# A diagonal of reciprocal roots in the opening, and a quarter of the first weights ahead of the last x tile

## The chip, the cores and the metric

The kernel runs on one core of one Trainium2 chip. The metric is the device time of one execution in microseconds; the median of three runs of the kernel before is 443.52 us (443.51 to 444.15).

## What is computed

A decoder layer on 512 tokens of width 1024, in float32. It begins with an RMSNorm and one wide projection, to which the change belongs:

```python
def rmsnorm(x, g):
    xf = x.astype(jnp.float32)
    y = xf * lax.rsqrt(jnp.mean(xf * xf, axis=-1, keepdims=True) + RMS_EPS)
    return (y * g.astype(jnp.float32)).astype(x.dtype)

h = rmsnorm(x, norm_g)
proj = jnp.einsum('bsd,dc->bsc', h, w_in)
```

Behind it stand dilated window attention for three groups of four heads, block-sparse attention for eight heads, gates, two branch projections, an output projection, a residual add and a last RMSNorm.

## The kernel before

Tokens lie in four x tiles of 128 rows (`TT` = 4). The projection wants them turned, as eight pieces of 128 channels by 512 tokens (`KT_D` = 8). Each operand of a projection is kept as a high part, rounded to the matmul's fast float32 form, and a low part, the rest; a product is three matmuls: high by high (L766), high by low weights (L767), low by high (L770). For the x side the parts are `hT_hi` and `hT_lo`, for the weights `w_hi` and `w_lo`.

The program is written engine by engine; each engine runs its instructions in the written order and waits on counters. A `link` is an instruction behind which the same engine waits for its own result.

The opening. SP issues the loads: the four x tiles (L570), the first chunk of weights in two column halves of 128 (L617, L618), then whole chunks of 256 columns (L620) into three buffers `raw`. ScalarE's queue loads 24 small vectors into `vecs` (the norm's gains and the biases). GpSimd makes the unit matrix `ident`, then eight instructions of distance constants (L666 to L683: iota and select), and then works on the first weights: rounding of rows 0 to 3 of the eight k pieces (L690), of rows 4 to 7 (L691), the low part of the latter (L693), the rounding of step 1 (L697). TensorE runs 14 full float32 matmuls of `ident` (L738), each of them two records in the trace.

For each x tile ScalarE sums the squares (L1010; of the last tile only the lower half, the upper is VectorE's, L1219), VectorE takes mean and reciprocal (L1205, L1206, L1228, L1230), ScalarE the root (L1015), and then the tile is scaled in place by that number per row: tiles 0 and 1 by VectorE (L1200), of tiles 2 and 3 the lower half by ScalarE (L1020) and the upper by VectorE. TensorE turns the scaled tile with eight transposes against `ident` (L750) into the PSUM banks. The vectors are turned by one transpose (L755) behind tile 0's; VectorE copies them out as `gb` and halves the biases into `hbias` (L1210, L1211). When tile 3 is turned, ScalarE writes `hT_hi` piece by piece (L1034), scaled by the gains, and VectorE `hT_lo` (L1241). Before that, VectorE makes the low part of k pieces 0 to 3 of the first weights (L1236).

The projection goes in steps of 128 columns, 24 matmuls of 512 columns each (L766 to L770), or for the values 48 of 256 (L816 to L818, two steps sharing their weights). Steps 0 and 1 are keys, 2 and 3 queries, 4 and 5 values. ScalarE rounds the weights of a step from step 2 on (L990), two steps ahead; GpSimd makes their low part (L662); ScalarE and VectorE take a finished key step (L1049, L1264) or query step (L1049, L1259). A load into a buffer waits until both parts of the chunk in it are made. From step 6 on attention work stands between the steps. VectorE finishes the constants with five instructions (L1437 to L1441) before its first step.

Of the kernel before, what the change touches and what calls it, by code (L numbers as in the profile page):

```python
# [29 lines left out]
F32 = mybir.dt.float32  # L30
# [6 lines left out]
P = 128  # L37
# [50 lines left out]
HALVED = 2  # L88
WARM = 14
NRING = 4  # L90
SKEW = 8
# [189 lines left out]
def hybrid_layer_program(nc, x, norm_g, w_in, b_merge, w_pa, w_pb, w_out, final_g, out):  # L281
    stats_dram = nc.dram_tensor("stats_by_position", (SEQ, NDIL * 8), F32, kind="Internal").ap()
    top = ExitStack()
    with top:
# [25 lines left out]
        ss_part = sb("ss_part", [P, 2], F32)  # L310
# [3 lines left out]
        rvar = sb("rvar", [P, TT], F32)  # L314
# [17 lines left out]
        squares = sb("squares", [P, TT, D], F32, xstack)  # L332
        xstack.close()
# [57 lines left out]
        first_half_in = [sem(f"first_half_in{i}") for i in range(2)]  # L391
# [5 lines left out]
        var_ready = sem("var_ready")  # L397
        rstd_ready = sem("rstd_ready")
        x_scaled = sem("x_scaled")
        x_scaled_low = sem("x_scaled_low")  # L400
# [66 lines left out]
        def raw_waits(item, half=0):  # L467

            if item == ("w", 0):
                return first_half_in[half], 16  # L470
# [97 lines left out]
        def _(sp):  # L568
            for i in range(TT):
                sp.dma_start(xs[:, i, :], x_t[:, i, :]).then_inc(x_in[i], 16)  # L570
            def place_values(u):

                V = V_odd if u % 2 else V_even
                sp.wait_ge(v_rows_ready, 2 * u)
                sp.wait_ge(valued, HU * (u - 1))
                for t in range(TT):
                    sp.dma_start(V[32 * t:32 * t + 32, :, :],
                                 V_rows[:, t, :]).then_inc(v_placed, 16)
# [10 lines left out]
            for n, (k, c) in enumerate(LOADS):  # L589
# [51 lines left out]
        def _(pool):  # L641
# [13 lines left out]
            def lows(n):  # L655
# [3 lines left out]
                if n >= NRING:  # L659
# [8 lines left out]
            link(nc.gpsimd.affine_select(out=d_full[:], in_=d_full[:], compare_op=ALU.is_ge, fill=BIG, base=384,  # L668
                                         pattern=[[-1, 512]], channel_multiplier=1))

            band = d_band[:].rearrange("p (a c) -> p a c", a=2)
            link(nc.gpsimd.iota(band, [[0, 2], [-1, 256]], base=P, channel_multiplier=1,
                                allow_small_or_imprecise_dtypes=True))
            link(nc.gpsimd.affine_select(out=band, in_=band, compare_op=ALU.is_ge, fill=BIG, base=P,
                                         pattern=[[0, 2], [-1, 256]], channel_multiplier=1))
            link(nc.gpsimd.affine_select(out=band, in_=band, compare_op=ALU.is_ge, fill=BIG, base=0,
                                         pattern=[[0, 2], [1, 256]], channel_multiplier=-1))

            link(nc.gpsimd.iota(d_quad[:], [[-4, P]], base=0, channel_multiplier=4,
                                allow_small_or_imprecise_dtypes=True))  # L680
            link(nc.gpsimd.affine_select(out=d_quad[:], in_=d_quad[:], compare_op=ALU.is_ge, fill=BIG, base=0,
                                         pattern=[[-1, P]], channel_multiplier=1))
            nc.gpsimd.iota(d_hex[:].bitcast(I32), [[-1, P]], base=0, channel_multiplier=1).then_inc(consts_ready, 1)  # L683
            pool.wait_ge(consts_ready, 2)

# [9 lines left out]
            pool.wait_ge(first_half_in[1], 16)  # L695
            src, kt = raw_half(1)
            nc.gpsimd.tensor_copy(ring(w_hi, 1, kt), src).then_inc(hi_ready, 1)  # L697

# [34 lines left out]
        def _(pe):  # L733
# [6 lines left out]
            for i in range(TT):  # L740
                if i < HALVED:
                    pe.wait_ge(x_scaled, i + 1)
                else:
                    pe.wait_ge(x_scaled_low, i - HALVED + 1)
                for k in range(KT_D):
                    if i >= HALVED and k == KT_D // 2:
                        pe.wait_ge(x_scaled, i + 1)
                    if i == 1 and k == 7:
                        pe.wait_ge(gb_ready, 1)
                    last = pe.transpose(ps[:, k, P * i:P * i + P], xs[:, i, P * k:P * k + P], ident[:, :])  # L750
                    if i == TT - 1:
                        last.then_inc(x_turned, 1)
                if i == 0:
                    pe.wait_ge(vec_in, 32)
                    pe.transpose(ps[:, 7, SEQ - 24:SEQ], vecs[:, :], ident[0:24, 0:24]).then_inc(vecs_turned, 1)  # L755
# [225 lines left out]
        def _(act):  # L981
# [26 lines left out]
            def square_rows(i, n):  # L1008
                act.wait_ge(x_in[i], 16)
                nc.scalar.activation(squares[:, i, 0:n], xs[:, i, 0:n], ACT.Square,  # L1010
                                     accum_out=ss[:, i:i + 1]).then_inc(squared, 1)

            def root(i):
                act.wait_ge(var_ready, i + 1)
                nc.scalar.activation(rstd[:, i:i + 1], rvar[:, i:i + 1], ACT.Sqrt).then_inc(rstd_ready, 1)  # L1015

            def scale_low_half(i):
                act.wait_ge(rstd_ready, i + 1)
                half = xs[:, i, 0:D // 2]
                nc.scalar.activation(half, half, ACT.Copy, scale=rstd[:, i:i + 1]).then_inc(x_scaled_low, 1)  # L1020

            for i in range(HALVED):
                square_rows(i, D)
                root(i)
            square_rows(2, D)
            square_rows(3, D // 2)
            for i in range(HALVED, TT):
                root(i)
            for i in range(HALVED, TT):
                scale_low_half(i)  # L1030
# [158 lines left out]
        def _(dve):  # L1189
# [8 lines left out]
            def scale_rows(i, at):  # L1198
                dve.wait_ge(rstd_ready, i + 1)
                nc.vector.tensor_scalar(xs[:, i, at:], xs[:, i, at:], rstd[:, i:i + 1], None,  # L1200
                                        ALU.mult).then_inc(x_scaled, 1)

            def variance(i):
                dve.wait_ge(squared, i + 1)
                link(nc.vector.tensor_scalar(var[:, i:i + 1], ss[:, i:i + 1], 1.0 / D, EPS, ALU.mult, ALU.add))  # L1205
                nc.vector.reciprocal(rvar[:, i:i + 1], var[:, i:i + 1]).then_inc(var_ready, 1)  # L1206

            def turn_vectors():
                dve.wait_ge(vecs_turned, 1)
                link(nc.vector.tensor_copy(gb[:], ps[:, 7, SEQ - 24:SEQ]))  # L1210
                nc.vector.tensor_scalar(hbias[:], gb[:, 8:24], 0.5, None, ALU.mult).then_inc(gb_ready, 1)  # L1211

            for i in range(HALVED):
                variance(i)
                scale_rows(i, 0)
            turn_vectors()
            last, high = TT - 1, slice(D // 2, D)
            dve.wait_ge(x_in[last], 16)
            link(nc.vector.scalar_tensor_tensor(out=squares[:, last, high], in0=xs[:, last, high], scalar=1.0,  # L1219
                                                in1=xs[:, last, high], op0=ALU.mult, op1=ALU.mult,  # L1220
                                                accum_out=ss_part[:, 0:1]))
            nc.vector.tensor_scalar(ss_part[:, 1:2], ss_part[:, 0:1], 1.0 / D, EPS, ALU.mult,
                                    ALU.add).then_inc(dve_chain, 1)
            chain[0] += 1
            variance(last - 1)
            dve.wait_ge(dve_chain, chain[0])
            dve.wait_ge(squared, last + 1)
            link(nc.vector.scalar_tensor_tensor(out=var[:, last:TT], in0=ss[:, last:TT], scalar=1.0 / D,  # L1228
                                                in1=ss_part[:, 1:2], op0=ALU.mult, op1=ALU.add))
            nc.vector.reciprocal(rvar[:, last:TT], var[:, last:TT]).then_inc(var_ready, 1)  # L1230
# [301 lines left out]
```

## Time and profile before

| | |
|---|---|
| median of 3 runs | 443.52 us |
| the profiled execution, own time | 443.48 us |
| its span, first to last instruction | 441.7 us |
| TensorE busy | 431.6 us, 98% of the span |
| VectorE, ScalarE, GpSimd busy | 212.8, 198.5, 176.3 us |
| first projection matmul starts | 14.58 us |

In the views PE is TensorE's matmuls, PEld its weight loads, DVE VectorE, ACT ScalarE, POOL GpSimd, SPq SP's DMA issues; L738 is line 738 of the kernel. A timeline row gives the start in us from the span's start, the duration in us, engine, line, operation, destination <- sources, shapes and count, and in brackets how long the engine was idle before it and what ended that. A DMA's landing is the time from issue to the arrival of the last byte.

### The profile page before, as it was taken

To read this page: it belongs to the slowest core of one execution; us is meant where nothing else is said; L and a number is where in the kernel's file an instruction comes from. 1 tells how busy PE (TensorE), PEld (TensorE's weight loads), DVE (VectorE), ACT (ScalarE), POOL (GpSimd) and SP (SyncE) were. 2 spreads that over 40 slices of the span, in tenths; PEclk is the share of its full clock that TensorE was granted. 3 is DMA by queue.
4 is the path that set the end of the run, shared out by engine and by line. 5 is a ranking of instruction groups with operands and counts; after the bars stand their busy time and mean duration, and the time that the engine had idled before them with its cause. 6 is when DMAs were issued, how large, how long until landed. Compare 5 with 4: busy or idle time off the path is not lost.

```text
span 441.7 us, 6258 instructions
## 1 busy us (share of the span) xinstructions
PE 431.6 (98%) x2377; PEld 374.5 (85%) x2377; DVE 212.8 (48%) x367; ACT 198.5 (45%) x401; POOL 176.3 (40%) x113
## 2 busy tenths in 40 slices
PE   7899999999999999999999999999999999999995
PEld 6789998899889988988888888888888888888885
DVE  3831244344435446757857664827025173083334
ACT  5743555335544464567555554533223543332111
POOL 4744442243243333646499543534355354200000
PEclk9999999999999999999999999999999999999999
DMA  8962234622452263024122022222222284210421
GB/s 284 286 192 96 96 96 83 159 96 95 91 150 97 96 168 110 25 96 143 49 95 96 0 73 96 96 72 96 95 71 96 95 261 156 113 66 0 149 90 47
DMA packets 40044, 48.31 MB, mean 109 GB/s; under 512 B 3768, under 2 KB 35536, under 8 KB 40016
## 3 DMA queue, kind: packets, MB, share of 16 engines
q1 hardware_dynamic: 37568, 47.72, 34.4%
q10 hardware_dynamic: 2448, 0.21, 0.4%
q8 instruction: 19, 0.31, 0.3%
q14 instruction: 9, 0.07, 0.1%
HBM read 39.48 MB, written 2.15 MB: 94 GB/s over the span
## 4 chain that ended last, share of the span: by engine, by line
PE 96%; DMA 2%; DVE 1%; ACT 1%; SPq 0%; issue 0%; DVEq 0%; ACTq 0%
PE ps L766 20%; PE ps L770 20%; PE ps L767 20%; PE ps L816 4%; PE ps L818 4%; PE ps L817 4%; PE ps L890 3%; PE ps L974 3%; PE ps L975 3%; PE ps L973 3%; PE ps L873 3%; PE ps L917 3%; PE ps L907 2%; DMA xs<-in_x 2%; PE ps L865 1%; PE ps L850 0%
## 5 line engine op out<-in xcount | busy, mean ns | idle before, releaser
L662 POOL TENSOR_TENSOR w_lo<-raw,w_hi 128x1024 fp32r<-128x1024 f32 (+1 forms) x59 | 138.1, 2342 | 175.4 <-ACT w_hi L990 175.4
L766 PE MATMUL ps<-hT_hi,w_hi 128*128 128x512 f32 x336 | 135.0, 402 | 1.1 <-DVE hT_lo L1241 1.1
L770 PE MATMUL ps<-hT_lo,w_hi 128*128 128x512 f32 x336 | 131.2, 390 | 0.0
L767 PE MATMUL ps<-hT_hi,w_lo 128*128 128x512 f32 x336 | 131.1, 390 | 0.0
L770 PEld LDWEIGHTS ps<-hT_lo,w_hi 128*128 128x128 f32 x336 | 63.1, 188 | 13.5
L766 PEld LDWEIGHTS ps<-hT_hi,w_hi 128*128 128x128 f32 x336 | 63.2, 188 | 11.2 <-issue 1.3
L767 PEld LDWEIGHTS ps<-hT_hi,w_lo 128*128 128x128 f32 x336 | 63.3, 188 | 9.9
L990 ACT CAST w_hi<-raw 128x1024 fp32r<-128x1024 f32 (+1 forms) x58 | 59.2, 1020 | 8.3 <-PE ps L770 5.4
L816 PE MATMUL ps<-w_hi,hT_hi 128*128 128x256 f32 x160 | 45.6, 285 | 0.0
L818 PE MATMUL ps<-w_lo,hT_hi 128*128 128x256 f32 x160 | 44.7, 279 | 0.0
L817 PE MATMUL ps<-w_hi,hT_lo 128*128 128x256 f32 x160 | 44.6, 279 | 0.0
L704 POOL TENSOR_TENSOR probs<-probs,frec 128x128 f32<-128x128 f32 (+3 forms) x32 | 22.1, 722 | 23.7 <-DVE frec L1307 23.7
L1102 ACT ACTIVATE probs<-probs,stats 128x128 f32<-128x128 f32 (+1 forms) x48 | 20.1, 419 | 24.1 <-DVE stats L1366 24.1
L816 PEld LDWEIGHTS ps<-w_hi,hT_hi 128*128 128x128 f32 x160 | 30.2, 188 | 0.1
L817 PEld LDWEIGHTS ps<-w_hi,hT_lo 128*128 128x128 f32 x160 | 30.1, 188 | 0.1
L1076 ACT ACTIVATE gate<-ps,hbias 128x512 f32<-128x512 f32 x16 | 11.0, 690 | 42.7 <-PE ps L770 42.5
L818 PEld LDWEIGHTS ps<-w_lo,hT_hi 128*128 128x128 f32 x160 | 30.1, 188 | 0.0
L1102 ACT ACTIVATE probs<-probs,fmin 128x128 f32<-128x128 f32 (+3 forms) x32 | 17.9, 560 | 26.2 <-DVE fmin L1366 26.2
L1049 ACT ACTIVATE QTs<-ps 64x512 fp32r<-64x512 f32 x20 | 11.9, 593 | 25.6 <-PE ps L770 25.2
L1264 DVE TENSOR_TENSOR KTs<-ps,KTs 64x512 fp32r<-64x512 f32 x20 | 13.8, 688 | 19.0 <-ACT KTs L1049 18.7
L890 PE MATMUL ps<-ident,probs 128*128 128x128 f32 x140 | 21.4, 272 | 0.0
L1247 DVE TENSOR_TENSOR wo_a_lo<-raw,wo_a_hi 128x1024 fp32r<-128x1024 f32 x5 | 6.7, 1377 | 30.1 <-ACT wo_a_hi L1000 30.1
(148 smaller groups left out, 665.6 us busy)
## 6 DMA issues: line engine op xcount, KB each, us to landing
raw<-in_w_in SPq DMA_DIRECT2D x25, 1024.0 KB, 4.9
KTs<-KTs SPq DMA_DIRECT2D x20, 256.0 KB, 3.4
raw<-in_w_out SPq DMA_DIRECT2D x4, 1024.0 KB, 4.8
xs<-in_x SPq DMA_DIRECT2D x4, 512.0 KB, 5.3
raw<-in_w_pb SPq DMA_DIRECT2D x4, 512.0 KB, 4.1
res<-in_x SPq DMA_DIRECT2D x4, 512.0 KB, 3.9
out<-weighted SPq DMA_DIRECT2D x8, 256.0 KB, 2.1
raw<-in_w_in SPq DMA_DIRECT2D x2, 512.0 KB, 8.9
```

The source lines that it names most:

```text
L662: nc.gpsimd.tensor_tensor(ring(w_lo, n, kt), src, ring(w_hi, n, kt).bitcast(F32), ALU.subtract).then_inc(lo_ready, 1)
L704: nc.gpsimd.tensor_tensor(row, row, frec[:, h.n - NDIL * HU, i:i + 1].broadcast_to([P, n]), ALU.mult).then_inc(normed, 1)
L766: pe.matmul(out, wh, hh, start=(k == 0), stop=False)
L767: pe.matmul(out, wl, hh, start=False, stop=False)
L770: return pe.matmul(out, wh, hl, start=False, stop=(k == kts - 1))
L816: pe.matmul(o, hh, wh, start=(k == 0), stop=False)
L817: pe.matmul(o, hl, wh, start=False, stop=False)
L818: last = pe.matmul(o, hh, wl, start=False, stop=(k == KT_D - 1))
L890: last = pe.transpose(ps[:, TURN_BANKS[bank], P * b:P * b + P], probs[:, h.n % 2, at:at + P], ident[:, :])
L990: nc.scalar.copy(ring(w_hi, n, kt), src).then_inc(hi_ready, 1)
L1102: nc.scalar.activation(row, row, ACT.Exp, bias=nmin(h, i), scale=-1.0, accum_out=row_sum(h, i)).then_inc(exp_ready, 1)
L1264: nc.vector.tensor_tensor(lo, src, hi.bitcast(F32), ALU.subtract).then_inc(k_low, 1)
```

## The change

The x tiles are no longer scaled. Every tile's squares are split between ScalarE (lower half) and VectorE (upper half); VectorE turns its sum into a part of the mean, ScalarE takes the root with the other part as scale and that part as bias, VectorE takes the reciprocal and writes a matrix `diag` with it on the diagonal (for the last tile ScalarE writes it). TensorE turns and scales a tile at once by full float32 matmuls of the tile with `diag` in place of transposes with `ident`. The vectors are turned right behind the 14 matmuls, ahead of tile 0. Of tile 2 the last two pieces are turned between those of tile 3. The first column half of the first weights is loaded in two parts of four k pieces: one ahead of the last x tile, one behind it. GpSimd's distance constants are made behind the low part of step 2 instead of at the start, VectorE's five finishing instructions behind the taking of step 2.

```diff
@@ sync
+            def load_first_half(m):
+
+                ks = slice(FIRST_K * m, FIRST_K * m + FIRST_K)
+                at = CHUNKS[0][1]
+                dst = raw[:, 0, :].rearrange("p (k c) -> p k c", k=KT_D)
+                sp.dma_start(dst[:, ks, 0:P], w_in_t[:, ks, at:at + P]).then_inc(first_in[m], 16)
+
             for i in range(TT):
+                if i == TT - 1:
+                    load_first_half(0)
                 sp.dma_start(xs[:, i, :], x_t[:, i, :]).then_inc(x_in[i], 16)
+            load_first_half(1)
...
                     if n == 0:
-                        sp.dma_start(dst[:, :, 0:P], w_in_t[:, :, at:at + P]).then_inc(first_half_in[0], 16)
-                        sp.dma_start(dst[:, :, P:256], w_in_t[:, :, at + P:at + 256]).then_inc(first_half_in[1], 16)
+                        sp.dma_start(dst[:, :, P:256], w_in_t[:, :, at + P:at + 256]).then_inc(first_in[2], 16)
@@ gpsimd
-            link(nc.gpsimd.iota(d_full[:], [[-1, 512]], base=384, channel_multiplier=1,
-                                allow_small_or_imprecise_dtypes=True))
...
-            pool.wait_ge(first_half_in[0], 16)
+            pool.wait_ge(first_in[0], 16)
             nc.gpsimd.tensor_copy(hi[:, low_k, :], src[:, low_k, :]).then_inc(first_hi, 1)
+            pool.wait_ge(first_in[1], 16)
             nc.gpsimd.tensor_copy(hi[:, high_k, :], src[:, high_k, :]).then_inc(hi_ready, 1)
...
                 lows(n)
+                if n == CONST_STEP:
+                    distances()
@@ tensor
-            for i in range(TT):
-                if i < HALVED:
-                    pe.wait_ge(x_scaled, i + 1)
-                else:
-                    pe.wait_ge(x_scaled_low, i - HALVED + 1)
-                for k in range(KT_D):
...
-                    last = pe.transpose(ps[:, k, P * i:P * i + P], xs[:, i, P * k:P * k + P], ident[:, :])
+            pe.wait_ge(vec_in, 32)
+            pe.transpose(ps[:, 7, SEQ - 24:SEQ], vecs[:, :], ident[0:24, 0:24]).then_inc(vecs_turned, 1)
+            def scaled_turn(i, k):
+
+                return pe.matmul(ps[:, k, P * i:P * i + P], xs[:, i, P * k:P * k + P], diag[:, i, :],
+                                 start=True, stop=True)
+
+            for i in range(TT - 1):
+                pe.wait_ge(diag_ready, i + 1)
+                for k in range(KT_D if i < TT - 2 else FIRST_TURNS):
+                    if i == 0 and k == KT_D - 1:
                         pe.wait_ge(gb_ready, 1)
+                    scaled_turn(i, k)
+            pe.wait_ge(last_diag, 1)
+            for k in range(KT_D):
+                scaled_turn(TT - 1, k).then_inc(x_turned, 1)
+                if FIRST_TURNS + k < KT_D:
+                    scaled_turn(TT - 2, FIRST_TURNS + k)
@@ scalar
+            for i in range(TT):
+                low = slice(0, D // 2)
                 act.wait_ge(x_in[i], 16)
+                nc.scalar.activation(squares[:, i, low], xs[:, i, low], ACT.Square,
                                      accum_out=ss[:, i:i + 1]).then_inc(squared, 1)
...
+                act.wait_ge(squared, i + 1)
+                act.wait_ge(part_ready, i + 1)
+                nc.scalar.activation(var[:, i:i + 1], ss[:, i:i + 1], ACT.Sqrt, scale=1.0 / D,
+                                     bias=ss_mean[:, i:i + 1]).then_inc(rms_ready, 1)
+            act.wait_ge(last_root, 1)
+            nc.scalar.activation(diag[:, TT - 1, :], ident[:, :], ACT.Copy,
+                                 scale=rstd[:, TT - 1:TT]).then_inc(last_diag, 1)
@@ vector
+            def square_rows(i):
+                high = slice(D // 2, D)
+                dve.wait_ge(x_in[i], 16)
+                link(nc.vector.scalar_tensor_tensor(out=squares[:, i, high], in0=xs[:, i, high], scalar=1.0,
+                                                    in1=xs[:, i, high], op0=ALU.mult, op1=ALU.mult,
+                                                    accum_out=ss_part[:, i:i + 1]))
+                nc.vector.tensor_scalar(ss_mean[:, i:i + 1], ss_part[:, i:i + 1], 1.0 / D, EPS, ALU.mult,
+                                        ALU.add).then_inc(part_ready, 1)
+
+            def root_diagonal(i):
+                dve.wait_ge(rms_ready, i + 1)
+                if i == TT - 1:
+                    nc.vector.reciprocal(rstd[:, i:i + 1], var[:, i:i + 1]).then_inc(last_root, 1)
+                    return
+                link(nc.vector.reciprocal(rstd[:, i:i + 1], var[:, i:i + 1]))
+                nc.vector.tensor_scalar(diag[:, i, :], ident[:, :], rstd[:, i:i + 1], None,
+                                        ALU.mult).then_inc(diag_ready, 1)
+
+            dve.wait_ge(consts_ready, 1)
+            for i in range(TT):
+                square_rows(i)
+                root_diagonal(i)
+                if i == 0:
+                    dve.wait_ge(vecs_turned, 1)
+                    link(nc.vector.tensor_copy(gb[:], ps[:, 7, SEQ - 24:SEQ]))
+                    nc.vector.tensor_scalar(hbias[:], gb[:, 8:24], 0.5, None, ALU.mult).then_inc(gb_ready, 1)
...
             for s in range(NS):
                 if s:
                     take_step(s - 1)
+                if s == CONST_STEP + 1:
+                    finish_constants()
```

`FIRST_TURNS` is 6, `CONST_STEP` 2, `FIRST_K` 4 as before.

## Rows read from the trace of the kernel before

**Rows 1.** The page, busy time of each engine with its share of the span.

```profile
PE 431.6 (98%) x2377; PEld 374.5 (85%) x2377; DVE 212.8 (48%) x367; ACT 198.5 (45%) x401; POOL 176.3 (40%) x113
```

**Rows 2.** TensorE's waits, whole span: us in total, times, longest.

```profile
PE ps L766 <- DVE hT_lo L1241: 1.1, 1, 1.1
```

**Rows 3.** Chain of waits, 0 to 16 us: start, duration, what.

```profile
0.74 0.39 SPq L570
...
2.12 7.07 DMA xs<-in_x
9.21 0.71 DVE squares L1219 x2
...
11.54 1.22 PE ps L750 x9
...
12.84 0.70 ACT hT_hi L1034
...
14.58 0.47 PE ps L766
```

**Rows 4.** Transfers of the four x tiles, by tile.

```profile
DMA to landing us min/median/max: 3.6/5.3/7.1
```

**Rows 5.** Timeline of GpSimd and VectorE, 5 to 21 us.

```profile
5.87 0.24 POOL L683 IOTA d_hex<- 128x128 int32 x1
...
11.12 0.86 POOL L690 CAST w_hi<-raw 128x512 fp32r<-128x512 f32 x1 [5.01 <-DMA raw<-in_w_in]
...
11.93 0.62 POOL L691 CAST w_hi<-raw 128x512 fp32r<-128x512 f32 x1
12.02 1.07 DVE L1236 TENSOR_TENSOR w_lo<-raw,w_hi 128x512 fp32r<-128x512 f32 x1 [0.51 <-POOL w_hi L690]
...
18.59 2.39 POOL L662 TENSOR_TENSOR w_lo<-raw,w_hi 128x1024 fp32r<-128x1024 f32 x1 [0.90 <-ACT w_hi L990]
...
18.84 2.23 DVE L1437 TENSOR_SCALAR d_hex<-d_hex 128x128 int32<-128x128 int32 x1
```

**Rows 6.** Timeline, VectorE and ScalarE, roots and squares.

```profile
5.75 0.16 DVE L1206 RECIPROCAL rvar<-var 128x1 f32<-128x1 f32 x1
...
5.95 0.20 ACT L1015 ACTIVATE rstd<-rvar 128x1 f32<-128x1 f32 x1 [0.42 <-DVE rvar L1206]
...
9.21 0.69 DVE L1219 SCALAR_TENSOR_TENSOR squares<-xs 128x512 f32<-128x512 f32 x1 [0.31 <-DMA xs<-in_x]
...
9.95 0.15 DVE L1222 TENSOR_SCALAR ss_part<-ss_part 128x1 f32<-128x1 f32 x1
```

**Rows 7.** By line: count, ns min/median/max, starts; then a timeline row.

```profile
L1184 ACT ACTIVATE rms<-out_ss,mean x4: 294/296/297, 407.2 to 437.5; 128x1 f32<-128x1 f32 x4
...
L1441 DVE TENSOR_SCALAR pT_hi<-ident x1: 228/228/228, 21.7 to 21.7; 128x128 fp32r<-128x128 f32 x1
...
51.12 0.40 ACT L1102 ACTIVATE probs<-probs,stats 128x128 f32<-128x128 f32 x1 [0.45 <-DVE stats L1366]
```

**Rows 8.** Timeline, TensorE and VectorE, around the turned vectors.

```profile
7.00 1.09 PE L750 MATMUL ps<-ident,xs 128*128 128x128 f32 x8
...
8.02 0.24 PE L755 MATMUL ps<-ident,vecs 24*128 24x24 f32 x1
8.51 0.18 DVE L1210 COPY gb<-ps 128x24 f32<-128x24 f32 x1
...
8.72 0.17 DVE L1211 TENSOR_SCALAR hbias<-gb 128x16 f32<-128x16 f32 x1
```

**Rows 9.** Warm-up: timeline, then by line, 1 to 3 and 6.2 to 7.2 us.

```profile
1.53 5.61 PE L738 MATMUL ps<-ident 128*128 128x128 f32 x28 [1.53 <-POOL ident L651]
...
L738 PE MATMUL ps<-ident x7: 421/421/580, 1.5 to 3.0; 128*128 128x128 f32 x7
...
L738 PE MATMUL ps<-ident x8: 275/275/398, 6.0 to 6.9; 128*128 128x128 f32 x8
```

**Rows 10.** Timeline, GpSimd and TensorE, where step 4 begins.

```profile
33.56 2.40 POOL L662 TENSOR_TENSOR w_lo<-raw,w_hi 128x1024 fp32r<-128x1024 f32 x1 [3.04 <-ACT w_hi L990]
...
36.44 0.28 PE L816 MATMUL ps<-w_hi,hT_hi 128*128 128x256 f32 x1
```

More of the change, by code:

```diff
@@ L87 @@
 FIRST_K = 4
-HALVED = 2
+FIRST_TURNS = 6
 WARM = 14
 NRING = 4
+CONST_STEP = 2
 SKEW = 8
@@ L309, in hybrid_layer_program @@
         ss = sb("ss", [P, TT], F32)
-        ss_part = sb("ss_part", [P, 2], F32)
+        ss_part = sb("ss_part", [P, TT], F32)
+        ss_mean = sb("ss_mean", [P, TT], F32)
         out_ss = sb("out_ss", [P, len(GROUPS)], F32)
@@ L390, in hybrid_layer_program @@
         raw_in = [sem(f"raw_in{i}") for i in range(NRAW)]
-        first_half_in = [sem(f"first_half_in{i}") for i in range(2)]
+        first_in = [sem(f"first_in{i}") for i in range(3)]
         const_step = sem("const_step")
@@ L396, in hybrid_layer_program @@
         dve_chain = sem("dve_chain")
[L397 to L400, printed above, removed]
+        part_ready = sem("part_ready")
+        rms_ready = sem("rms_ready")
+        diag_ready = sem("diag_ready")
+        last_root = sem("last_root")
+        last_diag = sem("last_diag")
         first_hi = sem("first_hi")
@@ L694, in _, with distances @@
                                     ALU.subtract).then_inc(lo_ready, 1)
-            pool.wait_ge(first_half_in[1], 16)
+            pool.wait_ge(first_in[2], 16)
             src, kt = raw_half(1)
             nc.gpsimd.tensor_copy(ring(w_hi, 1, kt), src).then_inc(hi_ready, 1)
+            def distances():
+                link(nc.gpsimd.iota(d_full[:], [[-1, 512]], base=384, channel_multiplier=1,
+                                    allow_small_or_imprecise_dtypes=True))
+                link(nc.gpsimd.affine_select(out=d_full[:], in_=d_full[:], compare_op=ALU.is_ge, fill=BIG, base=384,
+                                             pattern=[[-1, 512]], channel_multiplier=1))
+                band = d_band[:].rearrange("p (a c) -> p a c", a=2)
+                link(nc.gpsimd.iota(band, [[0, 2], [-1, 256]], base=P, channel_multiplier=1,
+                                    allow_small_or_imprecise_dtypes=True))
+                link(nc.gpsimd.affine_select(out=band, in_=band, compare_op=ALU.is_ge, fill=BIG, base=P,
+                                             pattern=[[0, 2], [-1, 256]], channel_multiplier=1))
+                link(nc.gpsimd.affine_select(out=band, in_=band, compare_op=ALU.is_ge, fill=BIG, base=0,
+                                             pattern=[[0, 2], [1, 256]], channel_multiplier=-1))
+                link(nc.gpsimd.iota(d_quad[:], [[-4, P]], base=0, channel_multiplier=4,
+                                    allow_small_or_imprecise_dtypes=True))
+                link(nc.gpsimd.affine_select(out=d_quad[:], in_=d_quad[:], compare_op=ALU.is_ge, fill=BIG, base=0,
+                                             pattern=[[-1, P]], channel_multiplier=1))
+                nc.gpsimd.iota(d_hex[:].bitcast(I32), [[-1, P]], base=0, channel_multiplier=1).then_inc(consts_ready, 1)
+                pool.wait_ge(consts_ready, 2)
             def normalise(h):
@@ L1196, in link @@
                 dve.wait_ge(dve_chain, chain[0])
[L1198 to L1229, printed above, removed]
@@ L1230, in _ @@
-            nc.vector.reciprocal(rvar[:, last:TT], var[:, last:TT]).then_inc(var_ready, 1)
-            for i in range(HALVED, TT):
-                scale_rows(i, D // 2)
+            def square_rows(i):
[6 more added lines that the diff above has]
+                                        ALU.add).then_inc(part_ready, 1)
@@ L1432, in merge, with finish_constants @@
                                         ALU.subtract).then_inc(mrg_lo_ready, 1)
-            dve.wait_ge(consts_ready, 2)
-            apart = d_hex[:].bitcast(I32)
-            link(nc.vector.tensor_scalar(apart, apart, 3, None, ALU.bitwise_and))
-            link(nc.vector.tensor_scalar(d_hex[:], apart, 1.0, BIG, ALU.min, ALU.mult))
-            link(nc.vector.tensor_tensor(d_hex[:], d_hex[:], d_quad[:], ALU.max))
-            for t in (pT_hi, pT_lo):
-                link(nc.vector.tensor_scalar(t[:, T_ZERO:T_ZERO + P], ident[:], 0.0, None, ALU.mult))
+            def finish_constants():
+                dve.wait_ge(consts_ready, 2)
+                apart = d_hex[:].bitcast(I32)
+                link(nc.vector.tensor_scalar(apart, apart, 3, None, ALU.bitwise_and))
+                link(nc.vector.tensor_scalar(d_hex[:], apart, 1.0, BIG, ALU.min, ALU.mult))
+                link(nc.vector.tensor_tensor(d_hex[:], d_hex[:], d_quad[:], ALU.max))
+                for t in (pT_hi, pT_lo):
+                    link(nc.vector.tensor_scalar(t[:, T_ZERO:T_ZERO + P], ident[:], 0.0, None, ALU.mult))
             for s in range(NS):
```

45 lines of the change are left out of this document (1 added, 44 removed).

## Prediction

> **What bounds the kernel now.** I read the page's busy shares first [rows 1]: TensorE is busy 98% of a span of 441.7 us. Then TensorE's own waits over the whole span [rows 2]: there are four groups, none after 15 us, the last in time being 1.1 us for the first `hT_lo`. From there on it never stands still. So the kernel is an opening that ends when the first projection matmul starts (L766 at 14.58 us) and 427 us of a full TensorE behind it. A change to the opening is worth what it moves that start, and the shift goes through to the end, unless a later cover breaks. The chain of waits [rows 3] shows what sets 14.58: the last x tile lands at 2.12 + 7.07 = 9.19, then squares at 9.21, root, scaling, nine transposes from 11.54, the first `hT_hi` (12.84), the first `hT_lo`, the first matmul (14.58). From the start of `hT_hi` to the matmul are 14.58 - 12.84 = 1.74 us, which the change leaves alone.
>
> **The load order.** SP now issues a quarter of the first weight chunk (256 KB) before the last x tile and the next quarter behind it. x tiles land every (7.1 + 2.1 - 3.6 - 0.7)/3 = 1.6 us [rows 3, 4]. The first half chunk (512 KB) came to GpSimd at 11.12 [rows 5], 1.93 us behind the last x tile, so a quarter costs about 0.93: the last x tile lands at 10.1 instead of 9.19, the first quarter at about 8.5, the second at 11.1 as before (the bytes ahead of it are the same). If the order cost nothing, 9.2; I take 10.1. Each issue on SP takes about 0.4 us [rows 3] while the queue is several us behind, so the added instruction hides there.
>
> **The new chain of one tile.** VectorE and ScalarE each square half of every tile. With S as the start of VectorE's squares: its sum is out at S + 0.74 and scaled at S + 0.89 [rows 6]; ScalarE's half runs at the same time and ends by then; 0.04 for the handover; the root. Before, the opening's root without a bias took 0.20 [rows 6]; the new one has a bias, as the root at the end of the kernel has, 0.30 [rows 7], so I take 0.30 (bounds 0.20 and 0.30). Then 0.03 and a reciprocal of 0.16 [rows 6], 0.04, and the diagonal begins at S + 1.46. On VectorE that is 0.23 for 128x128 [rows 7]; its next instruction begins some 0.08 before the end (an estimate: casts L690 and L691 overlap by 0.05, [rows 5]), at S + 1.61. So one tile costs VectorE 1.61 us in series, because it waits in order for ScalarE's root; the root's two bounds give 1.51 and 1.61. That is as long as a tile's landing takes.
>
> **Where the row of tiles starts.** Tile 0 lands at 0.74 + 3.6 = 4.34 [rows 3, 4] and its diagonal is ready near 6.1. Then VectorE waits for the turned vectors, and these stand behind the 14 warm-up matmuls on TensorE: the first instruction after those, a transpose, begins at 7.00 [rows 8]. The turning takes 0.24 and the handover 0.1, so VectorE resumes at 7.35; `gb` and `hbias` take 0.21 and about 0.14 more [rows 8], and tile 1's squares start at 7.70, although its data came near 6. What is queued behind that wait is every later square. Tile 2: 9.31. Tile 3: 10.92. The last x tile, landed at 10.1, is not late, so the weight quarter ahead of it costs nothing in this case; the VectorE row of tiles is late instead.
>
> **From tile 3 to the first matmul.** S = 10.92; its reciprocal is ready at 12.34, ScalarE makes the diagonal: a 128x128 activation with operands from a tile takes 0.40 [rows 7], bounds 0.23 (as VectorE) and 0.40. TensorE can start at 12.83. Is it free? A warm-up matmul leaves two records, a transpose one. Of the warm-up's 28 records 20 start between 1.53 and 6.0, 0.225 apart and 421 ns long, which is the lower level of 1.2 GHz; the last take 275 ns [rows 9], as the transposes' records do at 2.4 GHz, 0.11 apart (7 gaps and a last record of 0.27 in 1.09 us, [rows 8]). So a turn with the diagonal costs 0.22 to 0.23. Tile 0: 7.25 to 9.1; tile 1 from 9.4 to 11.25; six of tile 2 from 11.25 to 12.6: free just in time. The first turn of tile 3 reaches ScalarE after 0.11 + 0.27 + 0.1 = 0.48, at 13.31, and 1.74 later the matmul starts: 15.05. VectorE's low part of the first weights (1.07 before, [rows 5]) runs from 12.3 to 13.4, or to 14.1 behind GpSimd, while `hT_hi` is made until 14.0; hidden, at worst 0.1. Removed are the scalings of x and 2 us of idle TensorE; they buy 1.0 us of path after the last squares, which the later S more than spends: 15.05 - 14.58 = +0.47.
>
> **What moves behind the opening.** GpSimd's eight constants, 4.6 us that ended at 6.1, now stand between the low parts of steps 2 and 3. The low part of step 2, 20.98 before [rows 5], ends near 21.5, that of step 3 4.6 + 2.4 later at 28.5, and step 3 begins at 15.05 + 3 x 5.46 = 31.4 (four steps took 36.44 - 14.58 before, [rows 10]): covered by 2.9. The load waiting on that low part is issued 3 us later, and its weights are read over 10 us after; a key copy behind it on SP is read by the scores of step 6, past 45. VectorE's five finishing instructions move to 33.8, beside the low part of step 5 on GpSimd, which ends 0.48 before step 4 needs it [rows 10]. If they hold GpSimd back by one or two of their 0.23, the slack still covers it; three would cost 0.2. Cost 0, at worst +0.3.
>
> Sum: 443.48 (the profiled execution; span 441.7 and 1.8 around it, 0.04 from the median 443.52) + 0.47 = 443.95, told as 444.0.
>
> **A rule against this change.** Row first: VectorE's two-input subtraction L1236 took 1.07 for a shape that takes 0.69 in the squares, with GpSimd's cast beside it; GpSimd's cast took 0.86 beside VectorE's scaling and 0.62 alone; a 128x128 operation of VectorE (L1437) took 2.23 and ended when GpSimd's did [rows 5, 6]. The Trainium skill, SBUF — State Buffer, section Who interferes with whom, says that VectorE and GpSimd share a port pair that is locked for a whole instruction, and the first to issue wins. By that rule, the trace agrees.
>
> **Rivals.**
> 1. GpSimd goes first. The second quarter lands at about 11.1 and GpSimd's cast (0.62) starts then; tile 3's squares start at 10.92. If the cast starts first, the squares end as L1236 did, about 0.55 after the cast's end, so some 0.7 later than alone. Start 15.75, +1.2, 444.7: slower. For: 0.2 us decides, and the warm-up's end varies with the moment at which TensorE reaches 2.4 GHz (1 us earlier or later moves it by 0.5). It decides from a warm-up end 0.2 later or a landing 0.2 earlier. Against: by my sum VectorE is ahead. Chance 0.27.
> 2. The landing bounds. If the warm-up ends earlier, or the tile's cycle is 1.51 and handovers shorter, S is the landing: 10.15, and the start 10.15 + 4.13 = 14.28, -0.3: 443.2. Chance 0.17.
> 3. The diagonal turns run at 0.45, as the warm-up's pairs of records do at 1.2 GHz [rows 9]: tile 0 to 10.8, tile 1 to 14.4, six of tile 2 to 17.1, first matmul near 19.4: 448.3. Against: TensorE was at 2.4 GHz after the warm-up and again after 1.8 us idle. Chance 0.03.
> 4. The change does not do what it says: the early quarter doesn't delay x, and VectorE isn't held by the vectors. S = 9.2 to 9.5, first matmul near 13.4 to 13.6, 442.4: faster. It needs both steps above wrong. Chance 0.05.
>
> For rival 3 the Trainium skill has TensorE: Matmul & The Clock Gate, section Terms: transpose mode is 4 times faster for FP32. A turn would then cost 0.44 even at the upper level and the time would be rival 3's. The late warm-up records speak for a factor of 2.
>
> **How the numbers follow.** The forecast (444.0, own range 443.6 to 444.3) has 0.48. A measurement can tell about 0.2%, 0.89 us, from no change. Faster by more: rival 4, 0.05. Within: forecast and rival 2 and a little of rival 1, 0.67. Slower: the most of rival 1 and rival 3, 0.28. The range from 443.0 to 444.9 takes in rivals 1 and 2 with 0.15 and 0.2 us for their terms, and leaves out 3, 4 and the ends.
>
> **What would show it.** In the new trace: last x tile landing at 10.1; a gap on VectorE from 6.1 to 7.35 ended by TensorE; squares of tiles 1, 2, 3 at 7.7, 9.3, 10.9, 1.61 apart; two records a turn, 0.11 apart; first matmul at 15.05; no wait of TensorE after it. Wrong if VectorE's third squares last over 1 us beside GpSimd's cast (rival 1), if they start on the landing (rival 2), if TensorE is busy without a gap until tile 3 (rival 3), or if step 4 starts late.

## The result and the profile after

Over twelve runs of each kernel the changed one has a median of 444.61 us (443.59 to 446.6), the kernel before 443.65 us (442.96 to 444.15). The ratio is 1.0024, with a 95% interval of 1.0015 to 1.0034: slower by about 1.0 us; the ratio is just past the 0.2% that a measurement tells, the lower end of its interval is not. The profiled execution took 444.81 us with a span of 443.0, against 441.7 before, and a mean granted clock of 1.0.

The page's busy times answer [rows 1], and TensorE's waits over the whole span answer [rows 2] (us in total, times, longest):

```profile
PE 435.1 (98%) x2409; PEld 378.2 (85%) x2409; DVE 213.7 (48%) x371; ACT 196.7 (44%) x400; POOL 176.5 (40%) x113
```

```profile
PE ps L753 <- POOL ident L662: 1.5, 1, 1.5
PE ps L759 <- ACT diag L1035: 0.5, 1, 0.5
PE ps L759 <- DVE diag L1219: 0.4, 1, 0.4
```

TensorE is 3.5 us busier: 32 more records, and less idle time in the opening. The wait for `hT_lo` is gone from the list. And yet the first projection matmul (now L783) starts later than in [rows 3]. The timeline of the opening, rows of VectorE, GpSimd, ScalarE and TensorE, shows why:

```profile
1.52 5.46 PE L753 MATMUL ps<-ident 128*128 128x128 f32 x28 [1.52 <-POOL ident L662]
...
6.91 0.24 PE L756 MATMUL ps<-ident,vecs 24*128 24x24 f32 x1
...
7.18 0.18 DVE L1228 COPY gb<-ps 128x24 f32<-128x24 f32 x1 [0.90 <-PE ps L756]
...
7.48 0.69 DVE L1207 SCALAR_TENSOR_TENSOR squares<-xs 128x512 f32<-128x512 f32 x1
...
8.21 0.15 DVE L1210 TENSOR_SCALAR ss_mean<-ss_part 128x1 f32<-128x1 f32 x1
8.46 0.29 ACT L1032 ACTIVATE var<-ss,ss_mean 128x1 f32<-128x1 f32 x1 [2.01 <-DVE ss_mean L1210]
...
8.82 0.61 POOL L680 CAST w_hi<-raw 128x512 fp32r<-128x512 f32 x1 [7.35 <-DMA raw<-in_w_in]
8.98 0.52 DVE L1219 TENSOR_SCALAR diag<-ident,rstd 128x128 f32<-128x128 f32 x1
...
9.43 0.68 DVE L1207 SCALAR_TENSOR_TENSOR squares<-xs 128x512 f32<-128x512 f32 x1
...
11.02 0.66 POOL L682 CAST w_hi<-raw 128x512 fp32r<-128x512 f32 x1 [1.60 <-DMA raw<-in_w_in]
...
11.13 1.10 DVE L1207 SCALAR_TENSOR_TENSOR squares<-xs 128x512 f32<-128x512 f32 x1
...
13.50 2.50 PE L759 MATMUL ps<-diag,xs 128*128 128x128 f32 x20 [0.54 <-ACT diag L1035]
14.08 4.16 ACT L1040 ACTIVATE hT_hi<-ps,gb 128x512 fp32r<-128x512 f32 x7 [0.64 <-PE ps L759]
...
15.82 0.48 PE L783 MATMUL ps<-hT_hi,w_hi 128*128 128x512 f32 x1
```

VectorE idles 0.90 us until the turned vectors come, which TensorE makes behind the warm-up. Only then does it square tiles 1, 2 and 3, at 7.48, 9.43 and 11.13. Twice it meets a cast of GpSimd: tile 1's diagonal takes 0.52 instead of 0.29, and tile 3's squares, which start 0.11 behind the cast, 1.10 instead of 0.69. The first projection matmul starts at 15.82 instead of 14.58, 1.24 later; the span is 1.3 longer. This start decides the time of the whole kernel: in 12 of the 14 profiled executions told of here, the own time less the start is between 428.85 and 429.05 us (the two others are e8 and e10, below). By this the median of 444.61 belongs to a start near 15.66 (an estimate). In this execution the x tiles landed as worked out, the last at 2.60 + 7.5 = 10.1, a microsecond before VectorE came to it (transfers of the x tiles, answering [rows 4]):

```profile
DMA to landing us min/median/max: 3.6/5.4/7.5
```

Where step 4 begins, as in [rows 10], the moved constants cost nothing: VectorE's operation waits for all of GpSimd's subtraction, GpSimd itself takes 2.44 instead of 2.40, and TensorE finds its weights 0.44 early.

```profile
34.84 2.44 POOL L673 TENSOR_TENSOR w_lo<-raw,w_hi 128x1024 fp32r<-128x1024 f32 x1 [3.04 <-ACT w_hi L1007]
...
35.06 2.37 DVE L1437 TENSOR_TENSOR d_hex<-d_hex,d_quad 128x128 f32<-128x128 f32 x1
...
37.72 0.28 PE L833 MATMUL ps<-w_hi,hT_hi 128*128 128x256 f32 x1
```

### The profile page after: what moved, and what is told of

Same layout as the page of the kernel before. It is cut to its first block, busy times and chain, and to the rows that moved or that the text cites. A ratio compares the mean times of both kernels' runs of the same rounds, so it can differ in the third digit from the quotient of the medians.

```text
span 443.0 us, 6330 instructions
## 1 busy us (share of the span) xinstructions
PE 435.1 (98%) x2409; PEld 378.2 (85%) x2409; DVE 213.7 (48%) x371; ACT 196.7 (44%) x400; POOL 176.5 (40%) x113
## 4 chain that ended last, share of the span: by engine, by line
PE 97%; DVE 1%; ACT 0%; issue 0%; POOL 0%; DVEq 0%; POOLq 0%; ACTq 0%
PE ps L783 20%; PE ps L787 20%; PE ps L784 20%; PE ps L833 4%; PE ps L835 4%; PE ps L834 4%; PE ps L907 3%; PE ps L992 3%; PE ps L990 3%; PE ps L991 3%; PE ps L890 3%; PE ps L934 3%; PE ps L924 2%; PE ps L753 1%; PE ps L882 1%; PE ps L759 1%
## 5 line engine op out<-in xcount | busy, mean ns | idle before, releaser
L783 PE MATMUL ps<-hT_hi,w_hi 128*128 128x512 f32 x336 | 135.1, 402 | 0.0
L783 PEld LDWEIGHTS ps<-hT_hi,w_hi 128*128 128x128 f32 x336 | 63.2, 188 | 9.8
L1261 DVE TENSOR_TENSOR KTs<-ps,KTs 64x512 fp32r<-64x512 f32 x20 | 13.8, 688 | 22.4 <-ACT KTs L1055 22.0
```

The costliest lines, as they stand in the source:

```text
L783: pe.matmul(out, wh, hh, start=(k == 0), stop=False)
L1261: nc.vector.tensor_tensor(lo, src, hi.bitcast(F32), ALU.subtract).then_inc(k_low, 1)
```

## The experiments

Medians of the kernel before were 443.56, 443.49 and 443.46 us in the three sets of runs below.

**e1: the wait for the vectors moved into a hole.** VectorE is idle after each tile's squares until ScalarE's root; there the two copies fit.

```diff
             for i in range(TT):
                 square_rows(i)
-                root_diagonal(i)
-                if i == 0:
+                if i == 1:
                     dve.wait_ge(vecs_turned, 1)
...
+                root_diagonal(i)
```

> The changed kernel with VectorE's wait for the turned vectors and its two copies moved from behind tile 0's diagonal to between the squares and the root of tile 1. Theory (VectorE's row of tiles is late because it stands behind the warm-up matmuls): tile 1's squares start at 6.2 instead of 7.48, tile 2's at 7.9, tile 3's on its landing at 10.1, before GpSimd's cast at 11.0, so they take 0.69 and not 1.10; the reciprocal is ready near 11.6, and now the 22 turns ahead of tile 3 end near 12.1: first projection matmul at 14.4 to 14.5 instead of 15.82, time 1.3 below the changed kernel, 443.3, or 0.2 to 0.4 below the kernel before. Rival (the early weight quarter or the longer turns set the time): tile 3 is not earlier, within 0.3 of the changed kernel.

443.26 us (442.8 to 444.24), ratio to before 0.9994 (0.9983 to 1.0004), which lies clear of the changed kernel's interval. The timeline of VectorE and TensorE:

```profile
5.87 0.68 DVE L1207 SCALAR_TENSOR_TENSOR squares<-xs 128x512 f32<-128x512 f32 x1
...
7.13 0.18 DVE L1227 COPY gb<-ps 128x24 f32<-128x24 f32 x1 [0.38 <-PE ps L756]
...
9.84 0.69 DVE L1207 SCALAR_TENSOR_TENSOR squares<-xs 128x512 f32<-128x512 f32 x1 [0.23 <-DMA xs<-in_x]
```

```profile
7.03 7.41 PE L759 MATMUL ps<-diag,xs 128*128 128x128 f32 x64
14.26 0.47 PE L783 MATMUL ps<-hT_hi,w_hi 128*128 128x512 f32 x1
```

Tile 3's squares now wait for their landing and take 0.69; the matmul starts at 14.26. The place of one wait, with the two meetings with GpSimd's casts that came of it, is worth the whole loss (that e1 is also 0.3 faster than the kernel before is not shown, its interval reaches 1.0004). It is shown that VectorE's row of tiles, held by the warm-up's end, set the time of the changed kernel.

**e2: the last x tile first.** Both quarters behind the four x tiles.

> The changed kernel with the last x tile loaded ahead of both weight quarters. Theory (VectorE's row is late, the landing is not): the last x tile lands at 9.2, a microsecond earlier, and that alone gives nothing; the first cast moves to 10.15, where it leaves tile 1's diagonal alone (0.29 instead of 0.52), so tile 3's squares start at 10.9 and are ahead of the second cast at 11.0: first matmul near 15.2, 0.2 to 0.6 below the changed kernel. Rival (the landing sets the time): 0.9 or more below the changed kernel.

444.14 us, ratio 1.0015 (1.0002 to 1.0027). In the profile tile 3's squares took 0.68 and the first matmul started at 14.61:

```profile
10.33 0.68 DVE L1206 SCALAR_TENSOR_TENSOR squares<-xs 128x512 f32<-128x512 f32 x1
10.58 0.91 POOL L679 CAST w_hi<-raw 128x512 fp32r<-128x512 f32 x1 [9.12 <-DMA raw<-in_w_in]
...
14.61 0.47 PE L782 MATMUL ps<-hT_hi,w_hi 128*128 128x512 f32 x1
```

Of the 1.21 that this start is earlier, 0.56 is that the vectors were turned at 6.35 in that execution instead of 6.91. The rest is that both meetings are missing: with all of x first, GpSimd's casts began at 10.58 and 11.44, too late for tile 1's diagonal (0.24 less from the turned vectors to tile 3's squares) and behind the start of those squares (0.41 less from there to the matmul). So in the changed kernel's execution the early weights did cost something, by the casts that they started, and not by a late x tile. The median is 0.5 lower, as expected, with intervals that overlap, and still above the kernel before: the load order is not the whole of the microsecond; that it is a part of it is likely and not proven.

**e3: GpSimd's second cast held.** It waits until VectorE has its part of tile 3's mean.

```diff
             pool.wait_ge(first_in[1], 16)
+            pool.wait_ge(part_ready, TT)
```

> The changed kernel with GpSimd's second cast made to wait for VectorE's part of tile 3's mean as well. Theory (VectorE waits for the whole of GpSimd's cast, 0.42 in the profile): tile 3's squares take 0.69 instead of 1.10, the first matmul starts at 15.4 instead of 15.8, 0.3 to 0.4 below the changed kernel, 444.2; GpSimd's later pieces are still in time (the low part of k pieces 4 to 7 by 14.5, needed at 18). Rival (the 1.10 is the price of the landing weights or chance, or the turns bound the end): no change, 444.6.

444.32 us, ratio 1.0017 (1.0007 to 1.0028). The squares took 0.68 and the matmul started at 14.82, partly since the vectors were turned at 6.57 and no cast met tile 1's diagonal:

```profile
10.55 0.68 DVE L1208 SCALAR_TENSOR_TENSOR squares<-xs 128x512 f32<-128x512 f32 x1
...
14.82 0.47 PE L784 MATMUL ps<-hT_hi,w_hi 128*128 128x512 f32 x1
```

What the meeting at tile 3 costs is read from the start of its squares to the first projection matmul: 4.69 in the changed kernel and in e4, where the squares took 1.10, and 4.27 or 4.28 in e2, e3 and e5, where they took 0.68. That is 0.42. The median of e3 moved by 0.3, the size expected; the intervals overlap, so by the runs this is a likely part and not a proven one.

**e4: the constants back at the start.**

> The changed kernel with GpSimd's distance constants and VectorE's five finishing instructions back where they stood before the change. Theory (their move costs nothing): TensorE has no wait after its first projection matmul in either form, and the time is that of the changed kernel, 444.6, within 0.3. Rival (the move brings GpSimd and VectorE into each other's way near step 4, or delays a load): 0.3 or more below the changed kernel.

444.38 us, ratio 1.0021 (1.0008 to 1.0034), first matmul at 15.89, tile 3's squares 1.10 again (they began at 11.20, the cast at 11.07). Their move neither costs nor brings anything that can be measured.

**e5: three warm-up matmuls fewer.** `WARM = 11` in the changed kernel.

> The changed kernel with 11 warm-up matmuls instead of 14, nothing else. Theory (VectorE's row of tiles hangs on the warm-up's end): six records of 0.113 fewer, VectorE resumes 0.6 to 0.7 earlier, tile 3's squares start near 10.4 to 10.5, ahead of GpSimd's second cast, so the 0.42 of waiting goes too: first matmul 0.9 to 1.1 earlier than in the changed kernel's profile, median about 443.7. Rival (the load order sets the end): no change, 444.5. If fewer warm-up matmuls leave TensorE at its lower level longer, the turns of tile 0 show 421 ns and the gain is smaller.

443.74 us (443.28 to 444.6), ratio 1.0001 (0.9988 to 1.0014): the loss is gone, as expected. The profile, of an execution that took 444.27, shows less than was expected. The vectors were turned at 6.42, only 0.49 earlier, since nearly all of the warm-up's records still had the lower level's 421 ns. And the weights landed earlier too (GpSimd's second cast at 10.41), so the collision fell on tile 2's diagonal instead; the first matmul started 0.52 earlier, not 0.9 to 1.1:

```profile
10.41 0.62 POOL L682 CAST w_hi<-raw 128x512 fp32r<-128x512 f32 x1 [1.52 <-DMA raw<-in_w_in]
```

```profile
10.39 0.72 DVE L1219 TENSOR_SCALAR diag<-ident,rstd 128x128 f32<-128x128 f32 x1
```

```profile
15.30 0.47 PE L783 MATMUL ps<-hT_hi,w_hi 128*128 128x512 f32 x1
```

So it is the median that speaks for the warm-up's end, not this profile. The landing and the warm-up's end move by up to a microsecond and more between the profiled executions, so a near tie between GpSimd and VectorE can fall either way.

**e6 and e7: e1 with the last x tile first, and that with 11 warm-up matmuls.**

> The kernel of e1 with, besides, the last x tile loaded ahead of both weight quarters. Theory (once VectorE's row starts early, TensorE's 22 turns of two records ahead of tile 3 set the end): tile 3's squares start at 9.5, 0.3 earlier, yet TensorE is busy without a gap from 7.0 to the first projection matmul at 14.26, as in e1: same time, 443.3, within 0.2. Rival (the landing of the last x tile bounds e1): 0.3 or more below e1.

> The kernel of e6 with 11 warm-up matmuls. Theory (turns bound e1 and e6): the turns start near 6.4, 22 of them end near 11.4, tile 3's diagonal is ready at 11.4 too, first matmul at 13.8 to 13.9, 0.4 below e1: 442.8 to 442.9. Rival (something behind the turns bounds e1): 443.3.

e6: 443.11 us, ratio 0.999 (0.9978 to 1.0003). e7: 442.87 us (442.5 to 443.33), ratio 0.998 (0.9967 to 0.9993): the fastest of all, and the only one whose interval lies below the kernel before; its gain of 0.2% is at the limit of what a measurement tells. TensorE's rows, e6 first, then e7:

```profile
6.65 7.41 PE L758 MATMUL ps<-diag,xs 128*128 128x128 f32 x64
13.88 0.47 PE L782 MATMUL ps<-hT_hi,w_hi 128*128 128x512 f32 x1
```

```profile
6.75 7.83 PE L758 MATMUL ps<-diag,xs 128*128 128x128 f32 x64
14.40 0.47 PE L782 MATMUL ps<-hT_hi,w_hi 128*128 128x512 f32 x1
```

In e1 and e6 the turns run without a gap and the first projection matmul comes 7.23 behind the first turn in both, although tile 3's squares start at 9.84 in one and at 9.55 in the other. In e7's execution all 22 records of the warm-up and the first of the turns were still at the lower level of 1.2 GHz, so the turns began no earlier than in e6 and took 7.65; its start of 14.40 missed the expected 13.8. Its median was nevertheless as expected, and the profiled execution, 443.33, was the longest of the 12, so it was not a typical one; e6 against e7 stays within the noise.

**e8: the load order alone, in the old opening.**

> The kernel before with the new load order alone: a quarter of the first weights ahead of the last x tile and a quarter behind it. Theory: here the landing of the last x tile sets the chain, and it comes 0.9 later (10.1 instead of 9.2), so the first matmul starts 0.9 later, near 15.5, time 444.4. Rival (the quarter costs x nothing, or the earlier weights free VectorE's low part and give it back): within 0.3 of the kernel before, 443.6.

448.59 us (447.83 to 449.78), ratio 1.0112 (1.0091 to 1.0134): 5.1 slower, not 0.9. Timeline of GpSimd, of VectorE, of TensorE, then two stretches of 2 us (busy time of PE, PEld, VectorE, ScalarE and GpSimd, then the granted clock, the DMA engines' share and GB/s):

```profile
10.98 0.62 POOL L702 CAST w_hi<-raw 128x512 fp32r<-128x512 f32 x1 [1.54 <-DMA raw<-in_w_in]
11.68 1.27 POOL L704 TENSOR_TENSOR w_lo<-raw,w_hi 128x512 fp32r<-128x512 f32 x1
12.89 1.24 POOL L708 CAST w_hi<-raw 128x1024 fp32r<-128x1024 f32 x1
14.21 2.41 POOL L672 TENSOR_TENSOR w_lo<-raw,w_hi 128x1024 fp32r<-128x1024 f32 x1
```

```profile
11.71 2.69 DVE L1211 TENSOR_SCALAR xs<-xs,rstd 128x512 f32<-128x512 f32 x2
14.33 2.83 DVE L1247 TENSOR_TENSOR w_lo<-raw,w_hi 128x512 fp32r<-128x512 f32 x1
```

```profile
12.70 3.68 PE L761 MATMUL ps<-ident,xs 128*128 128x128 f32 x16 [3.30 <-ACT xs L1031]
18.09 0.77 PE L777 MATMUL ps<-hT_hi,w_hi 128*128 128x512 f32 x1 [1.71 <-ACT hT_hi L1045]
```

```profile
10.00:12.00 2.00, 0.00 (x0) 0.00 (x0) 1.85 (x8) 1.09 (x5) 0.94 (x2) 0.81 1.13 306
12.00:14.00 2.00, 1.30 (x6) 1.30 (x7) 2.00 (x2) 1.26 (x3) 2.00 (x2) 0.50 1.10 350
```

Two further things happened. GpSimd's four instructions ran back to back with the landed quarters while VectorE had its scalings and its low part to do; these waited for whole instructions of GpSimd, 2.69 for 0.88 of scaling and 2.83 for 0.69 of subtraction. And TensorE, idle for 3.30 us, fell to half the granted clock, the level of 1.2 GHz, and stayed there until after 21. The two can be priced: the first projection matmul starts 3.51 later than in the kernel before (18.09 against 14.58), and behind it the execution takes 430.5 instead of 428.9, 1.6 more, the price of the lower level.

**e10, e11, e12: the two effects apart, on e8.** e10 puts eight matmuls of `ident` into TensorE's wait for tile 2, e11 holds GpSimd's second cast until VectorE's low part is done, e12 has both.

```diff
+                    if i == HALVED:
+                        for _ in range(8):
+                            pe.matmul(ps[:, 0, P * i:P * i + P], ident[:, :], ident[:, :], start=True, stop=True)
...
             pool.wait_ge(first_half_in[1], 16)
+            pool.wait_ge(first_lo, 1)
```

> The kernel of e8 (the old opening with the new load order) with eight matmuls of the unit matrix on TensorE in its wait for the last two tiles, their result overwritten. Theory (in e8 the wait of 3.3 us took TensorE to its lower level, and VectorE's first low part stood behind GpSimd's whole subtraction): the transposes of tiles 2 and 3 take 2.0 instead of 3.7 and the first projection matmuls 0.23 instead of 0.43 apart, but the first one still starts near 18, held by VectorE's low part: 1.5 below e8, 447.0. Rival (the landing is worth all of it): no change against e8, 448.6.

> The kernel of e8 with GpSimd's second cast made to wait for VectorE's first low part. Theory (VectorE and GpSimd block each other for whole instructions): VectorE's two scalings take 0.9 instead of 2.7 and its low part 0.7 instead of 2.8; the idle stretch of TensorE is still 3 us, so it runs at the lower level: first matmul near 16.4 and 1.5 lost in the first steps, 446.8. Rival (the clock alone made e8 slow): within 0.5 of e8.

> The kernel of e8 with both: the eight matmuls of e10 and the held cast of e11. Theory (e8's 5.1 are 0.9 of later landing, about 1.5 to 2 of lower clock and 2.5 of blocking): only the landing is left, first matmul at 15.4, 0.9 above the kernel before, 444.4. Rival (a third cause): 445.5 or more.

e10: 448.34 us, ratio 1.0113 (1.0095 to 1.013), four runs. e11: 444.36 us (443.39 to 446.9), ratio 1.0023 (1.0007 to 1.0039). e12: 443.97 us (443.42 to 444.72), ratio 1.0011 (0.9999 to 1.0022). e10's gain did not come, and its rows say where it went: TensorE's transposes were fast, but the first matmul still waited 3.0 us for VectorE, and behind that wait the clock fell (to a granted 0.50 from 19 to 21), with the same 1.6 behind the first matmul as in e8:

```profile
12.66 2.41 PE L764 MATMUL ps<-ident,xs 128*128 128x128 f32 x16 [1.45 <-ACT xs L1034]
18.04 0.47 PE L780 MATMUL ps<-hT_hi,w_hi 128*128 128x512 f32 x1 [2.97 <-DVE hT_lo L1255]
...
19.41 0.63 PE L781 MATMUL ps<-hT_hi,w_lo 128*128 128x512 f32 x1
```

In e11 the blocking was gone and with it 4.2 us, more than the 1.8 expected: in the profiled execution TensorE's idle time was 2.2 us (tile 3 had landed at 9.4), and it kept the upper level. That was not so in all runs: five of the ten took 443.39 to 443.94 with a mean granted clock of 0.998 or 0.999, the other five 444.77 to 446.9 with 0.991 to 0.996. In e12, where the eight matmuls fill the wait, none is below 0.996 and none takes over 444.72.

```profile
10.79 0.88 DVE L1212 TENSOR_SCALAR xs<-xs,rstd 128x512 f32<-128x512 f32 x2
11.59 0.69 DVE L1248 TENSOR_TENSOR w_lo<-raw,w_hi 128x512 fp32r<-128x512 f32 x1
```

```profile
11.70 1.97 PE L762 MATMUL ps<-ident,xs 128*128 128x128 f32 x16 [2.18 <-ACT xs L1032]
```

From tile 3's squares to the first projection matmul the kernel before takes 5.37, e11 5.37 and e12 5.36, but e8 8.05 and e10 8.03. So the blocking is worth 2.7 of e8's loss, and 0.8 is tile 3's landing at 10.0 in e8's execution. The lower clock's 1.6 has no single cause: in e8 the granted clock fell between 11.0 and 11.5, before the scalings were held up; in e10, where that wait was filled, it fell behind the wait for VectorE; and e11's longer runs, without the blocking, show a lower mean clock too. With both covered, e12 is 0.5 above the kernel before by the medians, in the place of the 0.9 that I gave the later landing, but its interval reaches 0.9999, and in its profile tile 3 landed at 9.1: that the order makes x land later is not shown by it.

**e9: what the second record of a turn costs.** e1 with transposes in place of turns; the scaling by the reciprocal root is left out.

> The kernel of e1 with transposes against the unit matrix in place of the turns with the diagonal; every wait stays, the scaling of x by the reciprocal root is left out. Theory (two records a turn instead of one cost 0.113 each, and in e1 TensorE's 32 turns fill 7.03 to 14.26): the turns no longer bound, the chain through the last diagonal does: first turn of tile 3 at 11.8, hT_hi at 12.2, first projection matmul at 13.9, 0.3 below e1, 442.9. Rival (something else bounds e1): time of e1, 443.3.

443.54 us, ratio 0.9999 (0.9989 to 1.0009), no faster than e1: the expectation failed. Its execution doesn't decide it. There the vectors were turned at 7.53, and two tiles' squares met a cast, 1.10 each, so that VectorE was late and TensorE had gaps.

```profile
7.53 0.24 PE L756 MATMUL ps<-ident,vecs 24*128 24x24 f32 x1
7.69 2.04 PE L759 MATMUL ps<-ident,xs 128*128 128x128 f32 x16
10.75 0.87 PE L759 MATMUL ps<-ident,xs 128*128 128x128 f32 x6 [1.02 <-DVE diag L1218]
```

That TensorE's turns bound e1 and e6 is read from their gapless rows; that shorter turns would save time has not been shown.

## Why the prediction was right, and where it was short

The range (443.0 to 444.9) held the time, and the direction of the point, 444.0, was right; the point fell 0.6 short of 444.61, which lies outside the 443.6 to 444.3 given to the forecast's own mechanism and 0.1 from rival 1's 444.7. So the range held because it took in rival 1, a path with a chance of 0.27; 0.67 had been given to a time within 0.2% of the kernel before. By the profiled execution the sum was +0.47 and the trace has +1.24. Step by step:

- The load order. In this execution the last x tile came at 10.1 and the second quarter at 11.0, as predicted, and x was not late. The 10.1 was in part luck: in ten profiles with this order the last x tile landed between 9.1 (e12) and 10.1 (changed kernel, e4), in the four with all of x first between 9.2 and 9.5, so a cost of 0.9 per quarter is not shown. And "costs nothing" overlooked that a quarter that lands early starts a cast early: that cast met tile 1's diagonal. That the same order costs 5 us in the old opening (e8) I had not looked at.
- VectorE behind the warm-up. Right, and it is the cause: resumed at 7.18, predicted 7.35 (the warm-up ended 0.1 earlier, and the handover taken as 0.1 was 0.03); tile 1's squares at 7.48, predicted 7.70. e1 and e5 show it by taking the wait away or shortening it.
- The cycle of a tile. Mis-sized: 1.61 predicted, 1.70 without a collision (9.43 to 11.13) and 1.95 with one (7.48 to 9.43). ScalarE's root starts 0.10 after the part is ready, not 0.04, and the diagonal takes 0.29 with a scalar from a tile, not the 0.23 of a constant. With tile 1's collision of 0.23 this put tile 3's squares at 11.13 instead of 10.92.
- The tie at tile 3. This is the term that failed in this execution. I had VectorE 0.2 ahead of GpSimd's cast and gave the other order 0.27 as a rival; with the longer cycle GpSimd was ahead by 0.11, and the squares cost 0.42 more, not the 0.7 that I put on the rival. Both profiles of this opening as it stands (changed kernel and e4) have GpSimd first; that the tie falls both ways over the runs, which would put the median between forecast and rival, is argued and not shown.
- From tile 3 on. 0.10 more from the first turn to `hT_hi` (0.58), 0.04 more before it; the 1.74 to the matmul held. With the terms above: 15.05 + 0.21 + 0.42 + 0.04 + 0.10 = 15.82. The prediction's words that the missing scalings buy 1.0 us of path are a slip that its sum does not contain: from tile 3's squares to the matmul it was 5.37 before and 4.13 forecast, 1.24 less; measured are 4.27 without a collision and 4.69 with one.
- Two records a turn, 0.113 apart. Right: the 64 records of e1 begin within 7.13 us. The rival of 0.45 a turn is out, and with it the factor of 4 between a float32 turn and a transpose: 0.226 against 0.11 is a factor of 2.
- The moved constants. Right: e4 finds no difference, and step 4's slack was 0.44.

## What to carry to other kernels

In a kernel whose one full engine never waits again, look at which in-order queue makes the opening late: a cheap wait (here two copies behind a warm-up) costs everything that stands behind it, and costs nothing in a hole that is there anyway. When two engines exclude each other for whole instructions, a transfer that lands earlier can start the wrong one first; price every near tie both ways, and hold the one that has slack. And judge a reordered load in the opening where it will run: by the medians the same order cost half a microsecond at most beside the diagonals (e2) and 5 us beside the scalings (e8).

## What was not expected of the hardware

- The end of 14 warm-up matmuls moves by over a microsecond between executions: they ended at 6.28 in e8, 6.42 in e2, 6.98 in the changed kernel, 7.59 in e9 and 7.76 in e12. In each the records are 421 ns long at first and 275 ns later, and the change comes at a different moment: before 4.9 in e2, after 6.6 in e9. With 11 matmuls it came only after the warm-up in e7.
- In the profiled executions TensorE kept its granted clock over 1.8 us (before) and 2.2 us (e11) of idleness, lost it in 3.3 us of it (e8), and half a microsecond behind 3.0 us (e10). The kernel before did not always keep it: of its 93 runs in the three sets, 32 have a mean granted clock of 0.991 to 0.996 and a median of 444.29 us, the other 61 have 0.997 to 0.999 and 443.39. Of the changed kernel's 12 runs one has 0.996, and is its fastest; the others have 0.997 to 1.0. Against those 61 runs the changed kernel's median is 1.2 us longer, as its first matmul is later in the trace. No trace of such a run of the kernel before was kept, so where it lost the clock is not shown.
- One run of twelve of the changed kernel, of e2 and of e4 took 446.6 to 446.9 us, 2 us above the others, with a mean granted clock of 0.999 or 1.0. None of them was traced; the cause is open.
- VectorE's scalar_tensor_tensor that reads one tile through both inputs waits for GpSimd's cast like one with two tiles: 1.10 instead of 0.69. The Trainium skill, SBUF — State Buffer, section Who interferes with whom, describes such waiting for an instruction with both inputs in SBUF; here e8 agrees, with 2.83 us for a subtraction that took 0.69 in e11, where the cast was held. Instructions with one tile and a number per row as inputs waited too: the diagonals (0.52 in the changed kernel, 0.72 in e5, for 0.29) and the scalings of e8 (2.69 for 0.88).
